# Causal mask moved from TensorE to VectorE and GpSimd, with query blocks in descending order

## What is computed

```
h = rmsnorm(x, g_norm) * (1 + scale) + shift          # shift, scale, gate from c @ w_ada
q_sb, k_sb, v_sb, q_fx, k_fx, v_fx, g_path, f_logit = split(h @ w_in)
# stick-breaking heads (8 of 64 columns), causal is key < query (strict)
log_rem = where(causal, log_sigmoid(-z), 0)           # z = q.k / 8
a = where(causal, exp(log_sigmoid(z) + sum of log_rem over later keys), 0);  o_sb = a @ v
# forgetting heads (8 of 64 columns), causal is key <= query
logits = q.k / 8 + cum[query] - cum[key];  o_fx = softmax(where(causal, logits, -inf)) @ v
y = concat(rmsnorm(o_sb), rmsnorm(o_fx)) * silu(g_path)
out = rmsnorm(x + (1 + gate) * (y @ w_out), g_final)
```

## Time and profile before

| what | value |
|---|---|
| time, median of three | 832.02 us |
| span of the profiled execution, first to last instruction | 828.7 us |
| TensorE busy | 720.7 us, 87% |
| VectorE busy | 490.9 us, 59% |
| ScalarE busy | 408.4 us, 49% |
| GpSimd busy | 390.7 us, 47% |
| mean granted TensorE clock | 0.973 |

### The profile page before, as it was taken

One profiled execution on the slowest core, in us unless ns is written; L12 is line 12 of the kernel. 1 busy time (PEld: TensorE's weight loads), 2 busy tenths in 40 slices (PEclk: granted clock), 3 DMA queues, 4 the chain that ended last, 5 costly groups with the idle time before them and its releaser, 6 DMA issues.

```text
span 828.7 us, 10998 instructions
## 1 busy us (share of the span) xinstructions
PE 720.7 (87%) x3936; PEld 604.4 (73%) x3936; DVE 490.9 (59%) x993; ACT 408.4 (49%) x846; POOL 390.7 (47%) x325
## 2 busy tenths in 40 slices
PE   0257965989999999999989989998899899999996
PEld 0146754768887887888777878887788788788884
DVE  1486663776564567756634676565447765545565
ACT  4027333576457555554645555555556465623132
POOL 2244422535866563467476644665556465221100
PEclk9988997999999999999989999999999999999998
DMA  6553332104245431133342411244432308894223
GB/s 185 183 200 148 129 100 40 35 22 86 98 102 138 108 103 26 26 91 102 88 136 57 102 26 26 77 128 127 152 94 67 85 25 304 243 311 166 68 90 128
DMA packets 64390, 91.57 MB, mean 111 GB/s; under 512 B 5448, under 2 KB 39880, under 8 KB 63824
## 3 DMA queue, kind: packets, MB, share of 16 engines
q1 hardware_dynamic: 57216, 72.17, 30.4%
q0 software_dynamic: 5376, 14.68, 5.6%
q10 hardware_dynamic: 1744, 4.02, 1.2%
HBM read 67.23 MB, written 23.63 MB: 110 GB/s over the span
## 4 chain that ended last, share of the span: by engine, by line
PE 34%; DMA 21%; POOL 19%; issue 9%; DVE 9%; ACT 6%; SPq 1%; DVEq 0%; POOLq 0%; ACTq 0%
DMA w_raw<-in_w_in 15%; PE psum L1376 10%; POOL w_lo L540 6%; DMA work<-in_w_ada_t 5%; PE psum L1290 4%; PE psum L1291 4%; PE psum L1295 4%; PE psum L1364 4%; DVE work L1037 3%; PE psum L1342 3%; POOL w_hi L534 3%; POOL work L554 2%; POOL work L608 2%; DVE stacks L1005 2%; POOL work L614 2%
## 5 line engine op out<-in xcount | busy, mean ns | idle before, releaser
L1290 PE MATMUL psum<-h_hi,w_hi 128*128 128x512 f32 x496 | 209.6, 423 | 23.9 <-POOL h_lo L591 13.5
L1295 PE MATMUL psum<-h_hi,w_lo 128*128 128x512 f32 x496 | 197.6, 398 | 0.0
L1291 PE MATMUL psum<-h_lo,w_hi 128*128 128x512 f32 x496 | 197.2, 398 | 0.0
L800 ACT ACTIVATE pt_hi<-psum 128x512 fp32r<-128x512 f32 (+1 forms) x192 | 87.5, 490 | 140.5 <-PE psum L1342 137.3
L1097 DVE TENSOR_TENSOR pt_lo<-psum,pt_hi 128x512 fp32r<-128x512 f32 (+1 forms) x192 | 100.6, 551 | 84.4 <-ACT pt_hi L800 83.4
L608 POOL TENSOR_TENSOR work<-work 128x127 f32<-128x127 f32 (+3 forms) x64 | 77.4, 1211 | 152.2 <-DVE work L1037 152.2
L1290 PEld LDWEIGHTS psum<-h_hi,w_hi 128*128 128x128 f32 x496 | 96.0, 193 | 43.6 <-issue 16.2
L1037 DVE TENSOR_TENSOR_SCAN work<-work 128x128 f32<-128x128 f32 (+3 forms) x64 | 104.1, 1627 | 32.5 <-ACT work L768 32.4
L1342 PE MATMUL psum<-ident,work 128*128 128x128 f32 x576 | 88.8, 282 | 29.9 <-POOL work L614 16.0
L1295 PEld LDWEIGHTS psum<-h_hi,w_lo 128*128 128x128 f32 x496 | 95.5, 192 | 22.2
L1291 PEld LDWEIGHTS psum<-h_lo,w_hi 128*128 128x128 f32 x496 | 96.1, 194 | 16.6
(11 more groups left out here) (141 smaller groups left out, 1291.5 us busy)
## 6 DMA issues: line engine op xcount, KB each, us to landing
w_raw<-in_w_in SPq DMA_DIRECT2D x32, 512.0 KB, 9.4
work<-in_w_ada_t SPq DMA_DIRECT2D x24, 512.0 KB, 9.2
work<-in_x SPq DMA_DIRECT2D x16, 512.0 KB, 6.6
w_split_scratch<-work SPq DMA_DIRECT2D x16, 512.0 KB, 3.4
y_split_scratch<-work SPq DMA_DIRECT2D x10, 512.0 KB, 3.7
work<-forget_scratch SPq DMA_DIRECT2D x8, 512.0 KB, 5.1
work<-in_w_out SPq DMA_DIRECT2D x16, 256.0 KB, 5.6
stacks<-y_split_scratch POOLq DMA_DIRECT2D x4, 1024.0 KB, 6.7
```

The source lines that it names most:

```text
L800: nc.scalar.activation(pt_hi[:, a:e, (g % 2) * P:(g % 2 + 1) * P], bank, ACT.Copy).then_inc(s_thi, 1)
L1290: nc.tensor.matmul(bank, hi, h_hi[:, c_, cols], start=(c_ == 0), stop=False)
L1291: last = nc.tensor.matmul(bank, hi, h_lo[:, c_, cols], start=False, stop=(kind == "f" and c_ == DC - 1))
L1295: last = nc.tensor.matmul(bank, lo, h_hi[:, c_, cols], start=False, stop=(c_ == DC - 1))
```

## The change

The mask matmul L1318 is gone. Its work is done in three places instead:

- SB, VectorE: before the scan, the diagonal block of `R` (128 x 128) is set to 1 where it is not causal, with a maximum against `mask_f`. The scan then waits for it.
- SB, GpSimd: before the product, the diagonal block of `U` is set to 0 where it is not causal, with an `affine_select`.
- FX, VectorE: -1e30 is added in place to the diagonal block of the row `CUM` (`mask_forget`). This spoils the block for later units of the head, so the query blocks have to run from last to first.

So both heads of a pair now begin with width 8 and end with width 1. The V transposes of step 2 move to step 1. At the start of the attention, parts of the last first-stage projection are placed between the first two units' scores.

```
-        return g // STEPS, (g % STEPS) // TB, g % TB
+        return g // STEPS, (g % STEPS) // TB, TB - 1 - g % TB
...
-    V_STEPS = [STEPS - 2, 2]
+    V_STEPS = [STEPS - 2, 1]
...
             def sb_probs(g):
-                n = (g % TB + 1) * P
+                n = width(g)
+                diagonal = U[g % 2][:, n - P:n]
+                pool.wait_ge(s_sig, SB_PIECE[last_piece(g)])
+                nc.gpsimd.affine_select(out=diagonal, in_=diagonal, compare_op=ALU.is_gt, fill=0.0, base=0,
+                                        pattern=[[-1, P]], channel_multiplier=1).then_inc(s_umask, 1)
+                pool.wait_ge(s_umask, SB_UNIT[g])
                 pool.wait_ge(s_scan, SB_UNIT[g])
...
-            for u in range(N_FIRST, 2 * N_FIRST):
+            for u in range(N_FIRST, 2 * N_FIRST - 1):
                 proj_out(u)
...
             act.wait_ge(s_ada, 3 * DC)
             scores_out(0)
+            proj_out(2 * N_FIRST - 1)
             scores_out(1)
...
+            def mask_forget(g):
+                _, a, qb = unit(g)
+                diagonal = CUM[a][:, qb * P:(qb + 1) * P]
+                nc.vector.tensor_tensor(diagonal, diagonal, mask_f[:, 1, :], ALU.add).then_inc(s_cmask, 1)
...
+                    nc.vector.tensor_tensor(diagonal, diagonal, mask_f[:, 0, :], ALU.max).then_inc(s_rmask, 1)
+                    dve.wait_ge(s_rmask, SB_UNIT[g])
                     nc.vector.tensor_tensor_scan(...)
...
+                if (g + 1) % TB:
+                    mask_forget(g + 1)
...
-                    if diagonal:
-                        last = nc.tensor.matmul(bank[:, c1 - c0 - P:c1 - c0], ident_bf[:],
-                                                mask_bf[:, 0 if is_sb(g) else 1, :], start=False, stop=True)
...
-            pe.wait_ge(s_maskb, 2)
             proj(N_FIRST + 3, 0, DC - 2)
             scores(0)
+            proj(N_FIRST + 3, DC - 2, DC)
             scores(1)
-            proj(N_FIRST + 3, DC - 2, DC)
             transpose_v(0, 0)
```

More of the change, by code:

```diff
@@ L29, in hybrid_trunk_kernel @@
     fp32r = mybir.dt.float32r
-    bf16 = mybir.dt.bfloat16
     ALU = mybir.AluOpType
@@ L54, in unit, with width, last_piece, last_group @@
     def unit(g):
-        return g // STEPS, (g % STEPS) // TB, g % TB
+        return g // STEPS, (g % STEPS) // TB, TB - 1 - g % TB
+    def width(g):
+        return (unit(g)[2] + 1) * P
     def pieces(g):
-        n = (g % TB + 1) * P
+        n = width(g)
         return [(a, min(a + HALF, n)) for a in range(0, n, HALF)]
+    def last_piece(g):
+        return g, len(pieces(g)) - 1
     def tgroups(g):
-        n = g % TB + 1
+        n = unit(g)[2] + 1
         return [(a, min(a + 4, n)) for a in range(0, n, 4)]
+    def last_group(g):
+        return "T", g, len(tgroups(g)) - 1
     def numbered(events):
@@ L520, in _ @@
             pool.wait_ge(s_mask, 1)
-            nc.gpsimd.affine_select(out=mask_f[:, 0, :], in_=mask_f[:, 0, :], compare_op=ALU.is_gt, fill=MASKED,
+            nc.gpsimd.affine_select(out=mask_f[:, 0, :], in_=mask_f[:, 0, :], compare_op=ALU.is_gt, fill=1.0,
                                     base=0, pattern=[[-1, P]], channel_multiplier=1).then_inc(s_mask, 1)
@@ L1063, in values_out @@
                 a = (q // (TB // 2)) % 2
-                qb = (2 * q) % TB
+                qb = unit(2 * q + 1)[2]
                 dve.wait_ge(s_pvs, q + 1)
@@ L1360, in values @@
                     pe.wait_ge(s_pvd, q)
-                for k in range(qb + 2):
-                    c0 = 0 if k <= qb else P
+                for k in range(qb + 1):
+                    c0 = 0 if k < qb else P
                     for n, src in enumerate((pt_hi, pt_lo)):
                         last = nc.tensor.matmul(OUT[:, c0:2 * P], v_stack[:, p % 2, a, k, :], src[:, k, c0:2 * P],
-                                                start=(k == 0 and n == 0), stop=(k == qb + 1 and n == 1))
+                                                start=(k == 0 and n == 0), stop=(k == qb and n == 1))
                 last.then_inc(s_pv, 1)
```

43 lines of the change are left out of this document (22 added, 21 removed).

## The result

The changed kernel takes 866.26 us (858.0 to 873.17, 4 runs) against 832.89 us (829.75 to 833.78) for the kernel before. Its longest run, 873.17 us, counts as a slow one and is left out of the ratio, which is 1.0355, 95% interval 1.0283 to 1.0426. By the ratio it is 30 us slower (24 to 35). I had forecast 847 us, slower; the sign was right, the time lies above my range.

What follows compares the result with a forecast made beforehand. The attention was taken as TensorE-bound, with about 3 us of waits per SB pair. Masks -8, SB waits +21, pair 0 +2, FX pairs -2 and start +1.5 gave +14.5 on 832.0: 847 us, own range 838 to 858.

Steps and rivals of the forecast that it cites:

- FX pairs: Pairs 1, 3, 5, 7: new waits +7.4 us, shorter waits for GpSimd's products -9; together -2, bounds -7 and +4.
- Steps 8 and 10, T(0), T(3) of SB pairs: T(i) is step i's transposes: TensorE waits 3.3, 1.8, 1.2, 3.9 us; +7 us each in pairs 2, 4, 6.
- Masks: Removing 128 mask matmuls from TensorE takes 8 us off, bounds 5 and 12; nothing counts where TensorE waits.
- Added operations: Maxima and additions on VectorE, affine_selects on GpSimd: 17 and 18 us, mostly hidden; about 0.35 us per SB unit's chain.
- Rival 3: VectorE and GpSimd block each other more, in SB chains and wide scans: +12 us on top, about 860 us; chance 0.08.
- Pair 0: First pair: waits of steps 8 and 10 added, about 2.5 us round the forget sums kept; +2 us.
- Start: Before the attention: load of `w_raw` 3.4 us later, TensorE has more work before its 8.5 us wait; +1.5, bounds -1 and +4.

Runs made afterwards that it cites:

- e17: Changed kernel plus 520 satisfied waits (259 instructions) on TensorE at the start, making its program as long as that of the kernel before; 849.72 us, ratio 1.0210.
- e8: Changed kernel's masks on VectorE and GpSimd and old addresses of small, but SB pairs ascending as in the kernel before, FX pairs descending; 865.66 us, ratio 1.0379.
- e18: Kernel before without its mask matmuls, no masking in their place, plus 520 satisfied waits at TensorE's start to keep its program length; 829.32 us, ratio 0.9962.
- e1: Changed kernel with all masks and the waits for them taken out, descending order kept; 846.37 us, ratio 1.0161.
- e5: Changed kernel plus two unused SBUF tensors in the places of the two removed, restoring the old addresses; 860.88 us, ratio 1.0345.
- e2: Changed kernel's descending order with the mask matmuls of the kernel before back on TensorE, no masks on VectorE and GpSimd; 847.53 us, ratio 1.0157.
- Both edits of the order: Changed kernel with k bank's second part ahead of sigmoids and scan, and GpSimd's squaring ahead of step 3's product; with old addresses too, 847.4 us, ratio 1.0184.
- e13: Changed kernel plus 256 satisfied waits at TensorE's start, which became only 127 instructions, leaving the program still short; 863.65 us, ratio 1.0380.
- e9: Kernel before without its mask matmuls, nothing in their place, ascending order and VectorE's mask copies kept; 839.69 us, ratio 1.0049.
- e16: Changed kernel with each of the 128 VectorE mask operations replaced by a one-input multiplication by one; 858.02 us, ratio 1.0316.
- e10: Changed kernel plus 128 one-column matmuls, never read, on TensorE at the start; 865.62 us, ratio 1.0360.

## Why the prediction was right in sign and wrong in size

Measured against e17, whose loads are those of the kernel before, the sum holds: 18.0 us in the spans (846.7 - 828.7), 1.0210 in the timed runs, forecast +14.5. In part that is luck. With 1 us of the mask matmuls put down to each pair, the forecast was +18 for pairs 2, 4 and 6, -6 for the FX pairs and +2.5 for start and pair 0; measured are +22.4, -2.4 and -0.5, and -1.4 behind the last pair. Errors of both signs cancel. The terms:

- *Steps 8 and 10, T(0), T(3) of SB pairs.* Forecast 3.3, 1.8, 1.2 and 3.9 us (1 of it at T(1)); measured in pair 2 after: 3.11, 1.73, 1.30 and 3.33 + 1.01. In pair 2 of e17 TensorE's idle time rose by 6.4 us (78.32 - 75.23 = 3.1 to 85.99 - 76.49 = 9.5), forecast +7. Right, and by the causes named. (At T(1) my own figures, 2.1 less 1.4, give 0.7 and not the 1 us that I used.) What the sum doesn't tell is that the order is not needed for the loss: with the new masks, e8 loses as much in the SB pairs in the ascending order.
- *Their clock.* Absent from the sum. In pair 2 of e17 TensorE was busy 76.49 us; without mask matmuls and at clock 1.00 it is 74.01 (e18). So about 2.5 us per pair came on top. Pairs 2, 4 and 6 of e17 together: +22.4 us, where +21 less their share of the masks (3) had been forecast.
- *Masks.* Forecast -8. The matmuls' own time was right (75.23 to 74.01 us of busy time in pair 2, 1.2 us for 16), but e18 gained 3.2 us only, with an interval that just reaches my lower bound of 5: in pair 2 the length fell by 0.45 us, since TensorE then waited for the same chains. I had said that where it waits none of it counts, and took 8 of 12 all the same. Mis-sized.
- *Added operations.* Forecast as 0.35 us in each late chain. In pair 2 TensorE's waits sum to 8.8 us without them (e1) and 10.5 with them, as forecast; but the 128 VectorE operations took 71.4 us instead of 35, and all three kinds cost some 15 us with the late loads (e5 less e1). Rival 3 named the mechanism and gave it +12 and a chance of 0.08; it belonged into the sum. Its +12 does not follow from its own terms (64 x 0.3 is 19 alone), and its 860 us lie near the measurement only because the late loads came on top. With the early loads they come to less: 17.5 (e17) less 13.1 (e2) plus 3.2 (e18) is 7.6 us, if the matmuls are worth as much in the descending order, which no run shows with equal loads.
- *FX pairs.* -2 forecast; pairs 1, 3, 5 and 7 of e17 are 2.4 us shorter together. The waits for the products did fall (16.0 to 3.5 us after). But step 8 cost 1.8 us in pair 3, not 0.5, behind held additions, and part of the fall comes from other load times: with those of the kernel before, e17 still stands 9.3 us for L627.
- *Pair 0.* Forecast +2. In e17 it is 5.7 us shorter (84.3 against 90.0): the 8.5 us wait at T(3) is gone. T(0) comes 5.2 us later instead (125.3 against 120.1), since the scores of step 1 wait 8.9 us for the sigmoids. Both belong together, -0.5 us where +3.5 had been forecast.
- *Start.* This is the step that failed: "+1.5, bounds -1 and +4". T(16) came 20.7 us later in the trace after, 16.0 us in e5, and 0.5 us earlier in e17. The order does no harm there. The late start came from the loads, and these from the program's length. In the timed runs it is 1.0345 (e5) less 1.0210 (e17), 11 us, which with the 17.5 us of e17 makes the 28.7 us of e5; the changed kernel's own ratio is 30 us (24 to 35). Without these 11 us the time would have lain inside my range. That loads could change without any change to them was in no term and no rival.

No kernel here that keeps the masks beats the kernel before. Both edits of the order with the full filler would be the next to try (848 us with the late loads, less some 11 to 14, an estimate from e5, e13 and e17); it was not run.

## What to carry over

Work on a bound engine that is taken away where it waits is worth little (here 3.2 us of 7 to 12), and the chains that it leaves behind decide: sum the chains first, and price each new wait of 3 us with the clock that falls behind it (here 2.5 us per pair). Two changes that lengthen the same chains don't add: test each without the other before naming one as the cause. An instruction of VectorE that works within SBUF must be priced by the GpSimd instruction that runs beside it, not by its own duration. And when a change alters a program's length, compare the first loads of both traces before explaining anything: a pair of kernels that differ there isn't a pair.

## What the runs showed of the hardware

- Load times come in two sets, tied to the length of TensorE's program: the fifth `w_raw` load takes 12.3 us or 16.4, the sixteenth 11.6 or 5.8 (before, after), and in all kernels of a set the fifth takes 11.7 to 13.6 us or 15.6 to 18.1, the sixteenth 9.7 to 11.6 or 5.6 to 6.6. The late set isn't worse everywhere: of the two kernels without masks in ascending order, e18 needs 81.1 us for pair 3 and e9 79.2.
- VectorE operations of 128 x 128 within SBUF that met a GpSimd instruction ended 0.13 to 0.16 us after it (0.08 to 0.09 us with one input, e16); the longest took 2.5 us instead of 0.28. It goes both ways. GpSimd's affine_select and the scan of VectorE beside it:

```profile
138.60 2.01 POOL L617 TENSOR_SCALAR_AFFINE_SELECT work<-work 128x128 f32<-128x128 f32 x1
```

```profile
136.72 3.81 DVE L1062 TENSOR_TENSOR_SCAN work<-work 128x896 f32<-128x896 f32 x1
```

- Two satisfied waits in a row become one instruction on TensorE of 0.106 us; the 128 one-column f32 matmuls of e10 are 256 in the trace and took 54.8 us:

```profile
5.46 54.78 PE L1285 MATMUL psum<-ones,ident 128*128 128x1 f32 x256 [5.46 <-DMA ident<-in_identity]
```
